# Two output products of the second block opened three chunks at a time, under the last head of the stage before them

## The reference, cut to what matters

```python
def hybrid_layer(h, mem, ...):
    xn = rms_norm(h, mix_norm_g)
    q, k, v, g, xb, yb = split(xn @ w_in)
    ret = silu(g) * head_group_norm(chunkwise_retention(rotary(q), rotary(k), v), ret_gn_g)  # 8 heads of 128
    lru = rms_norm(rg_lru(xb, ...) * gelu(yb), lru_norm_g)                                   # 1024 wide
    h = h + concatenate([ret, lru], -1) @ w_out
    h = h + memory_cross_attention(rms_norm(h, xattn_norm_g), rms_norm(mem), w_xq, w_xk, w_xv, w_xo)
    h = h + peer_ffn(rms_norm(h, ffn_norm_g), ...)      # 8 heads, top 16 of 16384 experts
    return rms_norm(h, final_norm_g)
```

## Time and profile before

| | |
|---|---|
| median of 3 executions | 3423.21 us (3421.35 to 3424.57) |
| the profiled execution | 3423.62 us, of which its span is 3421.8 us |
| TensorE busy | 3110.3 us, 91% |
| VectorE, ScalarE, GpSimd busy | 1922.4, 1279.3, 362.9 us |
| mean granted TensorE clock | 0.979 of full |
| eight heads and LRU groups end, `w_out2` starts | 1776.15 us |
| memory attention ends, `w_xo` starts | 2001.88 us |
| `w_xo` ends, expert stage starts | 2095.75 us |

### The profile page before, as it was taken

How to read it: one execution, slowest core, us unless ns; L and a number is a source line. 1 busy time by engine, 2 the same in 40 slices (tenths; PEclk the granted TensorE clock), 3 DMA queues, 4 the chain that set the end, 5 groups by cost and what they waited for, 6 DMA issues and landing times.

```text
span 3421.8 us, 43470 instructions
## 1 busy us (share of the span) xinstructions
PE 3110.3 (91%) x18098; PEld 2424.4 (71%) x18098; DVE 1922.4 (56%) x2855; ACT 1279.3 (37%) x2353; POOL 362.9 (11%) x361
## 2 busy tenths in 40 slices
PE   8998999999999999999989999998897768777776
PEld 8887877999999999998979989444453223232322
DVE  6546455455555555676765444555555655555554
ACT  4425444444444445565544343222222222222221
POOL 1001000100000000200001001212132222222220
PEclk9989999999999999999989999999999999999999
DMA  7434444555555555644445445999999999999998
GB/s 219 147 116 158 161 139 148 201 178 184 184 185 185 182 181 181 214 161 160 161 161 183 149 148 208 432 430 430 431 420 430 431 425 431 431 431 430 431 430 343
DMA packets 93906, 911.08 MB, mean 266 GB/s; under 512 B 10312, under 2 KB 14792, under 8 KB 18572
## 3 DMA queue, kind: packets, MB, share of 16 engines
q0 software_dynamic: 37680, 540.03, 37.0%
q1 hardware_dynamic: 48816, 344.95, 29.3%
q10 hardware_dynamic: 7212, 23.30, 2.2%
HBM read 898.81 MB, written 9.44 MB: 265 GB/s over the span
## 4 chain that ended last, share of the span: by engine, by line
PE 68%; DMA 21%; DVE 6%; ACT 3%; issue 1%; ACTq 0%; POOL 0%; DVEq 0%; POOLq 0%
PE sums L551 15%; PE sums L553 15%; PE sums L552 15%; PE sums L963 10%; DMA area<-in_uv,cst 9%; DMA hT<-in_uv,cst 5%; DMA ringx<-in_uv,cst 4%; DMA ring<-in_uv,cst 2%; PE sums L919 2%; PE sums L575 2%; PE sums L577 1%; PE sums L576 1%; ACT cst L1008 1%; ACT area L1008 1%; DVE area L2076 1%
## 5 line engine op out<-in xcount | busy, mean ns | idle before, releaser
L1571 DVE TENSOR_TENSOR wl<-ring,wh 128x1024 fp32r<-128x1024 f32 x612 | 749.3, 1229 | 653.2 <-ACT wh L1008 652.5
L1008 ACT ACTIVATE wh<-ring 128x1024 fp32r<-128x1024 f32 x612 | 643.6, 1054 | 499.8 <-PE sums L553 443.7
L1008 ACT ACTIVATE cst<-cst 128x1 f32<-128x1 f32 (+2 forms) x786 | 234.3, 299 | 903.3 <-DVE cst L2076 843.4
L963 PE MATMUL sums<-area,cst 128*128 128x512 f32 x984 | 457.8, 611 | 99.7 <-ACT cst L1008 99.7
L963 PEld LDWEIGHTS sums<-area,cst 128*128 128x128 f32 x984 | 183.5, 193 | 355.6 <-issue 190.8
L2076 DVE CUSTOM_DVE_ANT_0 area<-area 128x2048 f32<-128x2048 f32 x123 | 281.7, 2291 | 257.6 <-DMA area<-in_uv,cst 257.6
L963 PE MATMUL sums<-ringx,cst 128*128 128x512 f32 x656 | 302.4, 606 | 62.6 <-ACT cst L1008 62.6
L551 PE MATMUL sums<-inputs,wh 128*128 128x256 f32 x1152 | 333.6, 290 | 11.9 <-DVE inputs L1604 7.5
L552 PE MATMUL sums<-inputs,wh 128*128 128x256 f32 x1152 | 327.5, 284 | 0.0
L553 PE MATMUL sums<-inputs,wl 128*128 128x256 f32 x1152 | 327.4, 284 | 0.0
L551 PE MATMUL sums<-normed,wh 128*128 128x256 f32 x1024 | 290.0, 283 | 0.0
(11 more groups left out here) (323 smaller groups left out, 5900.9 us busy)
## 6 DMA issues: line engine op xcount, KB each, us to landing
ring<-in_w_in_a SPq DMA_DIRECT2D x66, 1024.0 KB, 4.9
ring<-in_w_up SPq DMA_DIRECT2D x64, 1024.0 KB, 4.8
ring<-in_w_down SPq DMA_DIRECT2D x64, 1024.0 KB, 4.8
ring<-in_w_out SPq DMA_DIRECT2D x32, 1024.0 KB, 4.9
ring<-in_w_in_b SPq DMA_DIRECT2D x16, 1024.0 KB, 4.8
ring<-in_w_xk SPq DMA_DIRECT2D x16, 1024.0 KB, 5.1
ring<-in_w_xv SPq DMA_DIRECT2D x16, 1024.0 KB, 4.9
ring<-in_w_xq SPq DMA_DIRECT2D x16, 1024.0 KB, 4.9
```

The costliest lines, as they stand in the source:

```text
L963: mm = te.matmul(sums[t][:, 512 * i:512 * i + 512], diag[:, n % 2, :], v[:, 512 * i:512 * i + 512], start=False, stop=n % 128 == 127)
L1008: return sc.activation(out, in_, f, **kw)
L1571: ve.tensor_tensor(wl[:, j % 3, :], ring[:, load % 3, j % 2 * 1024:j % 2 * 1024 + 1024], wh[:, j % 3, :], ALU.subtract).then_inc(lo_in, 1)
```

## The change

- A new generator `three` makes the first three chunks of a product side by side: first the tiles `k` 0 to 7 of chunks 0, 1, 2 (six steps), then tiles 8 to 15 of chunks 0, 1, 2 (six steps). It takes three banks at its start. After tile 11 of chunk 0 it says `"?r7"` (for `w_out2`) or `"?m3"` (for `w_xo`). The weight arrays are laid out anew to fit.
- For `w_out2` it stands at the end of `projections2`, for `w_xo` at the end of `queries`. The chunks 3 to 15 follow alone.
- The inputs are split where they arise. The LRU result, now tiles 0 to 7, is split in three additional steps behind the LRU norm; head `h-1` is split in head `h`'s steps; the last head behind its last step, before `"+r7"`. In memory attention the four tiles of head `h-1` are split in head `h`'s transposes step, the last four before `"+m3"`.
- `uh`/`x1h` (for `w_out2`) and `uh`/`il` (for `w_xo`) take the splits. `uh` lies where the memory keys `kx` lie, so their load is issued in `w_xq`'s first chunk and no longer before `w_out2`'s splits.

The core of the diff (the bodies of `three` on ScalarE and VectorE are alike; the splits of VectorE answer those of ScalarE):

```diff
+            def three(hi, lo, where, gate):                      # TensorE
+                b = [bank_of() for c in range(3)]
+                for part in range(2):
+                    for c in range(3):
+                        j = half.n
+                        half.one()
+                        on.wait_ge(lo_in, j + 1)
+                        for k8 in range(8):
+                            k = 8 * part + k8
+                            if c == 0:
+                                split_ready(where, k)
+                            x = slice(k8 * P, (k8 + 1) * P)
+                            te.matmul(b[c][:, 0:T], wh[:, j % 3, x], hi[:, k, :], start=k == 0, stop=False)
+                            te.matmul(b[c][:, 0:T], wh[:, j % 3, x], lo[:, k, :], start=False, stop=False)
+                            mm = te.matmul(b[c][:, 0:T], wl[:, j % 3, x], hi[:, k, :], start=False, stop=k == 15)
+                            if k8 == 7:
+                                mm.then_inc(half_spent, 1)
+                            if k8 == 3:
+                                yield gate if part and c == 0 else None
+                        yield
 ...
                 for h in range(8):
                     yield from chunks3(3, ih, il, split_ready, "in2", f"h{h}")
+                yield from three(uh, x1h, "w_out2", "?r7")
 ...
                 norm_sums("lru")
                 yield
+                for j in range(3):
+                    yield
                 yield 2.2
                 yield "?v1"
                 permR = C("permR", 128)
                 for h in range(8):
                     yield f"?h{h}"
+                    if h == 7:
+                        yield 1.4
 ...
+                yield "+r7"
 ...
+                yield from three(uh, il, "w_xo", "?m3")          # queries
 ...
                     yield f"?x{h}"                               # memory
+                    if h == 3:
+                        yield 2.0
 ...
+                yield "+m3"
 ...
-            for _ in chunks3(16, ih, il, split_ready, "w_out2"):
+            for _ in chunks3(13, uh, x1h, split_ready, "w_out2"):
 ...
-            for _ in chunks3(16, il, ih, split_ready, "w_xo"):
+            for _ in chunks3(13, uh, il, split_ready, "w_xo"):
 ...
+                on.wait_ge(written, sum(WRITTEN["lru"]))         # ScalarE, recurrences
+                split(uh, xn, range(4))
+                yield
+                split(uh, xn, range(4, 8))
+                yield
+                yield
 ...
                     act(sg, g2[:, h, :], ACT.Sigmoid).then_inc(silu_in, 1)
                     yield
+                    if h:
+                        split(uh, xn, [7 + h])
                     yield
 ...
+                on.wait_ge(oh_in, 8)
+                split(uh, xn, [15])
+                yield "+r7"
 ...
                     act(PX[h % 2], banks[5][:, :], ACT.Copy).then_inc(xt_in, 1)
-                    yield
+                    if h:
+                        on.wait_ge(ox_in, 4 * h)
+                        split(uh, ox, range(4 * h - 4, 4 * h))
+                    yield
+                on.wait_ge(ox_in, 16)
+                split(uh, ox, range(12, 16))
+                yield "+m3"
 ...
-            sc.dma_start(kx, xk_d).then_inc(kv_in, 16)
             sc.dma_start(vx, xv_d).then_inc(kv_in, 16)
-            split(ih, xn)
-            on.wait_ge(xl_v, SPLIT_V["w_out2"] + 16)
 ...
+                    if h:                                        # VectorE, recurrences, third step of a head
+                        lower_of("w_out2", 7 + h, xn, uh, x1h)
 ...
+                    if h:                                        # VectorE, memory, transposes step
+                        for k in range(4 * h - 4, 4 * h):
+                            lower_of("w_xo", k, ox, uh, il)
```

More of the change, by code:

```diff
@@ L1088, in chunks3, with three @@
                     yield "+" + part if part and n == ns[-1] else None
+            def three(evict, gate):
+                for part in range(2):
+                    for c in range(3):
+                        next_half()
+                        yield gate if part and c == 0 else None
+                        if part:
+                            on.wait_ge(half_spent, half.n)
+                            evict(c)
+                        yield
             def spill_out(dst, width):
@@ L1253, in mixers, with split @@
                 split(oh_, oT)
-            def split(hi_, x):
-                for k in range(16):
+            def split(hi_, x, ks=range(16)):
+                for k in ks:
                     act(hi_[:, k, :], x[:, k, :], ACT.Copy).then_inc(xh_in, 1)
@@ L1297, in projections2 @@
                     yield from chunks3(range(3), None, f"h{h}")
+                yield from three(behind("w_out2", "xattn", ih, lambda n: G("xattn", n), xh_in), "?r7")
             def decay_rates():
@@ L1354, in recurrences, with load_keys @@
                     yield
+                on.wait_ge(oh_in, 8)
+                split(uh, xn, [15])
+                yield "+r7"
             def queries():
+                def load_keys():
+                    on.wait_ge(half_spent, 2 * PLAN.index(("w_xq", 0)))
+                    sc.dma_start(kx, xk_d).then_inc(kv_in, 16)
+                    root_rd(rd, RD_MEANS["xattn"])
                 for h in range(4):
-                    yield from chunks3(range(4), None, f"x{h}",
-                                       None if h else lambda: root_rd(rd, RD_MEANS["xattn"]))
+                    yield from chunks3(range(4), None, f"x{h}", None if h else load_keys)
+                yield from three(behind("w_xo", "ffn", xn, lambda n: G("ffn", n), xn_in), "?m3")
             def memory():
@@ L1469, in scalar @@
             on.wait_ge(o_mm, 8)
-            sc.dma_start(kx, xk_d).then_inc(kv_in, 16)
             sc.dma_start(vx, xv_d).then_inc(kv_in, 16)
-            split(ih, xn)
-            on.wait_ge(xl_v, SPLIT_V["w_out2"] + 16)
-            for _ in chunks3(range(16), behind("w_out2", "xattn", x1h, lambda n: G("xattn", n), xh_in)):
+            for _ in chunks3(range(3, 16), behind("w_out2", "xattn", ih, lambda n: G("xattn", n), xh_in)):
                 pass
@@ L1478, in scalar @@
             sc.dma_start(sk, A["sub_keysT"]).then_inc(keys_in, 16)
-            split(il, ox)
-            for _ in chunks3(range(16), behind("w_xo", "ffn", xn, lambda n: G("ffn", n), xn_in)):
+            for _ in chunks3(range(3, 16), behind("w_xo", "ffn", xn, lambda n: G("ffn", n), xn_in)):
                 pass
@@ L1875, in projections2 @@
                     yield from chunks3(range(3), qkg, f"h{h}")
+                yield from three(handed("w_out2", "w_xq", ih, ql, lambda n: G("xattn", n)), "?r7")
             def decay_rates():
@@ L1947, in recurrences @@
                 yield
+                yield
+                for j in range(2):
+                    for k in range(4 * j, 4 * j + 4):
+                        lower_of("w_out2", k, xn, uh, x1h)
+                    yield
                 yield 2.2
@@ L1992, in queries @@
                     yield from chunks3(range(4), xq, f"x{h}", None if h else lambda: factor("xattn"))
+                yield from three(plain("w_xo"), "?m3")
             def memory():
@@ L2012, in memory @@
                         ve.tensor_copy(ox[:, 4 * h + j, :], banks[6 + j % 2][:, 0:T]).then_inc(ox_in, 1)
+                for k in range(12, 16):
+                    lower_of("w_xo", k, ox, uh, il)
+                yield "+m3"
             def topk(g):
@@ L2121, in vector @@
             weave(recurrences(), projections2(), 3.9)
[L2122 to L2124 removed]
+            for _ in chunks3(range(3, 16), handed("w_out2", "w_xq", ih, ql, lambda n: G("xattn", n))):
                 pass
             weave(memory(), queries(), 4.0)
[L2127 to L2129 removed]
+            for _ in chunks3(range(3, 16), plain("w_xo")):
                 pass
@@ L2392 @@
     arrays["w_gates"] = g2
-    arrays["w_out2"] = chunks(I["w_out_2"][0])
+    arrays["w_out2"] = three(chunks(_np.concatenate([I["w_out_2"][0][1024:], I["w_out_2"][0][:1024]])))
     arrays["w_xq"] = chunks(I["w_xq_2"][0])
@@ L2396 @@
     arrays["w_xv"] = _np.stack([rows(I["w_xv_2"][0][:, 512 * p:512 * p + 512]) for p in range(4)])
-    arrays["w_xo"] = chunks(I["w_xo_2"][0])
+    arrays["w_xo"] = three(chunks(I["w_xo_2"][0]))
     arrays["w_pq"] = chunks(I["peer_w_q_2"][0])
```

19 lines of the change are left out of this document (16 added, 3 removed).

## The result

The changed kernel takes 3411.17 us (median of 7 runs, 3407.70 to 3417.52) against 3422.22 us for the kernel before on the same chip (7 runs, 3418.14 to 3427.10). The ratio is 0.9971, 95% interval 0.9959 to 0.9982: faster by 0.29%, or 9.9 us (6.2 to 14.0). The prediction said 7.0 us less than its own execution, 3416.6 us, with 3412.0 to 3421.5 as the range. The measured median lies 0.8 us under the lower end. The median of the kernel before differs between the two sets of runs as well (3423.21 and 3422.22 us), so the ratio is the fairer comparison: 0.9971 x 3423.21 = 3413.3 us, inside the range.

What follows compares the result with a forecast made beforehand. TensorE, busy 91% of the span, was taken as the bound, with gains only where it idles or runs slowly. 0.7 + 1.9 + 4.4 = 7.0 us off 3423.62 gave 3416.6 us, range 3412.0 to 3421.5.

Steps and rivals of the forecast that it cites:

- The order of the work: Tile 11 directly behind head 6's values, no `w_out2` matmul between head 7's steps; tile 15's wait ends 0.9 us earlier.
- Rival 4: `w_out2` work does fall under head 7 and covers 7.6 us more idle: 3409.0 us, chance 0.06.
- The first place: `w_out2` under the last LRU heads: 2.5 us saved less waits paid, net 0.7 us; slow clock stays.
- the bank wait: `three` taking three banks at once before head 6's rotation: 1.3 us paid, bounds 0.6 and 1.9.
- the late mean chain: A weight conversion on VectorE before head 6's mean correction delays the chain by 0.5 us, bounds 0 and 1.
- the 1.08 us for them: Saving from nine matmuls, chunk 0's tiles 12 to 14, run while TensorE waits for tile 15: 9 x 0.12.
- The second place: `w_xo` under memory attention's last head: idle 5.89 to 3.9 us, saving 1.9; clock stays up, giving back 4.4 us.
- Rival 1: The clock falls in memory attention's last head all the same, 1.5 us per fall: 3419.6 us with two, chance 0.23.
- the cost that the prediction weighed for them: By the skill's rule, bank waits would bring slow-clock stretches on top of their own length; 1.5 us per fall.
- The splits: Extra splits behind the LRU norm and in the heads stay hidden: cost 0, bounds 0 and 2 us; no gain.
- rivals 2 and 3: 2: paid waits cancel the saving, 3421 to 3424 us, chance 0.10. 3: VectorE late in head stage, 3426.2 us, chance 0.09.
- paid waits: The new bank wait and mean-chain delay before and in head 6, 1.3 and 0.5 us; without them 1.8 us less.

Runs made afterwards that it cites:

- experiment 7: Changed kernel with `three` begun later, so that its steps fall between head 7's: 3402.95 us against 3422.61, ratio 0.9945.
- the other execution: The changed kernel profiled once more with no edit: 3414.15 us.
- experiments 2 and 3: 2: kernel before with only operand buffers and key load moved, 3415.98 us. 3: changed kernel with other operand buffers in four `down` products, 3405.99 and 3411.07 us.
- Experiment 5: Changed kernel with each of the three chunks taking its bank when it begins, not all three at the start: 3411.00 us, one run.

## Why the prediction was right, and where it was not

**The order of the work: right.** Chunk 0's tile 11 stands directly behind head 6's values, and none of `w_out2`'s matmuls between head 7's steps except the nine behind the variance. Head 7's first wait is still 5.25 us at clock 0.50. The time from VectorE's last product (start of the multiply that writes head 7's output) to tile 15 fell from 2.34 to 1.39 us, 0.95 where 0.9 was written. The multiply before and after:

```profile
1773.81 0.42 DVE L1982 TENSOR_TENSOR xn<-area 128x256 f32<-128x256 f32 x1
1780.08 0.43 DVE L2067 TENSOR_TENSOR xn<-area 128x256 f32<-128x256 f32 x1
```

Rival 4 did not occur; experiment 7 shows what it would have been worth, 8.5 us where the prediction had 7.6.

**The first place: mechanism right, size wrong.** Forecast 0.7 us, measured 3.46. By terms:
- Idle time: 14.9 before, 12.68 after, 2.3 less. Within it the bank wait was 0.85 us, not 1.3, and the late mean chain cost 1.44 - 1.13 = 0.3, not 0.5.
- The slow clock: behind tile 15, 23 slow matmuls in place of 20, and the nine in front of it slow as well, which the 1.08 us for them had not counted: 12 x 0.096 = 1.2 us lost.
- The pace of `w_out2`: some 735 matmuls at full clock x 0.0033 = 2.4 us gained, or 1.6 at the 427 of the other execution.

Sum 2.3 - 1.2 + 2.4 = 3.5 us. The step that failed is the first sentence of that part, "The amount of matmul work is the same", from which I costed the new buffers of the operands at nothing. The amount is the same and its pace is not; experiments 2 and 3 show that it is the placement. The undisturbed products of before gave no sign of it: `up`, `down`, `w_out`, `w_out2` and `w_xo` all ran at 419. Only among the mixers' matmuls of the first 250 us did three of its product matmuls take some 0.356 us in place of 0.360, and whether that is the same effect was not tested.

**The second place: right.** Idle 5.89 to 3.66 us, 2.2 saved where 1.9 was forecast; each wait is near its sum: 0.70 (0.6), nothing before the transposes (0), 1.54 (1.8), 1.42 (1.5). The clock stayed at 1.00 from 1977.3 to 2000 us, so the values gave back 6.48 - 3.62 = 2.9 us, the start of `w_xo` the 1.5, and the transposes 0.85 - 0.64 = 0.2, which the forecast had only in its upper bound. Rival 1 did not occur. The Trainium skill's rule on cycling through PSUM banks (TensorE: Matmul & The Clock Gate, "A second HAM failure mode: psum-queue depth-cycling") speaks of waits that come again and again. Here there are two, far apart, of 0.85 and 0.70 us, and the 10 us behind the first and the 12 us around the second had clock 1.00: the cost that the prediction weighed for them did not appear, and waits in close succession are not tested by any run here.

```profile
1747.80:1757.80 10.00, 10.00 (x78) 1.00 0.56 195
1978.00:1990.00 12.00, 11.96 (x87) 1.00 0.45 167
```

Experiment 5 took them away, and what can be put down to that is their own length.

**The splits, rivals 2 and 3: right.** No row in the heads 0 to 5 has an idle time released by VectorE or ScalarE, and the wait behind the LRU norm is still 1.55 us.

**The sum.** 10.3 us in place of 7.0: 2.8 of the 3.3 us of difference are in the first place, and 1.6 to 2.4 of those are the pace. The profiled pair differs by more, 3423.62 - 3409.83 = 13.8 us, because the first execution of the changed kernel had 4.2 us of luck in the mixers. That the ratio's 3413.3 us lies inside the range is partly luck too: the pace was not among the range's terms. Its lower end had room for it because it allowed for no paid waits, of which 0.85 + 0.3 us came, and for an earlier return of the clock, which came later.

## What to carry to other kernels

When an edit moves an operand to another buffer, its matmuls may run at another pace: count the matmuls in an undisturbed stretch before and after, and try the free buffers for the longest product. Before a difference between two profiled executions is put down to a change, compare a fixed point upstream of it; 4 to 5 us arose there from the clock alone. Work laid under a chain covers only where it lies between the waits: seven steps under head 6 gained nothing but what stood at their edges, and the same steps under head 7 gained 8.5 us.

## What the runs showed of the hardware that was not expected

- With moving operands of 128x256 and the high and low product in turn, TensorE did 419 matmuls in 50 us at clock 1.00 in most placements, and 426 to 431 with the low part in `x1h`. As the place of the high part the same buffer gave 419. The cause is open.
- TensorE can be busy in 50.00 of 50 us, as the profile counts it, and still have the clock at 0.50 in part of them: the mean was 0.86 to 0.90 from 200 to 250 us in every execution. Products and the mixers' small matmuls alternate there; which of them the clock answers to was not tested. How long it lasts differed between executions of one kernel: 282 or 307 matmuls from 150 to 200 us, and 54.6 or 44.4 us at 0.50 in the first 1600.
- Waits of 0.5 to 1.6 us between dense stretches left the clock at 1.00 here, in both executions of the changed kernel; behind 5.25 us, and behind the 2.50 and 4.78 us of experiment 7, it was 0.50.
